# A sample's last tile routed ahead of the prompt's output products, and the prompt's choice of tokens folded into the sample's last rounds

## The reference, cut to what matters

```python
def expert_choice_ffn(x, w_router, w_gate, w_up, w_down):
    cap = EC_FACTOR * n_tok // N_EXPERTS              # 32 for the prompt, 128 for the sample
    aff = jax.nn.softmax((xf @ w_router).astype(jnp.float32), axis=-1)
    gate, idx = lax.top_k(aff.T, cap)
    xs = xf[idx]
    hdn = jax.nn.silu(jnp.einsum('ecd,edf->ecf', xs, w_gate)) * jnp.einsum('ecd,edf->ecf', xs, w_up)
    out = jnp.einsum('ecf,efd->ecd', hdn, w_down) * gate[..., None].astype(x.dtype)
    y = jnp.zeros_like(xf).at[idx.reshape(-1)].add(out.reshape(-1, D))
```

## Time and profile before

| | us |
|---|---|
| three runs | 3067.69, 3068.52, 3072.25 |
| median | 3068.52 |
| span of the profiled execution | 3067.2 |
| PE busy | 2904.8 |
| DVE busy | 2115.9 |
| ACT busy | 1578.3 |
| POOL busy | 500.5 |

### The profile page before, as it was taken

One profiled execution on the slowest core, in us unless ns is written; L12 is line 12 of the kernel. 1 busy time (PEld: TensorE's weight loads), 2 busy tenths in 40 slices (PEclk: granted clock), 3 DMA queues, 4 the chain that ended last, 5 costly groups with the idle time before them and its releaser, 6 DMA issues. The chain is left out here.

```text
span 3067.2 us, 50918 instructions
## 1 busy us (share of the span) xinstructions
PE 2904.8 (95%) x19782; PEld 2722.8 (89%) x19782; DVE 2115.9 (69%) x3420; ACT 1578.3 (51%) x2728; POOL 500.5 (16%) x477
## 2 busy tenths in 40 slices
PE   7999999989988899958999999999999999999997
PEld 5888888978877778848999999999999999999997
DVE  7212225767788566677778777877787778778887
ACT  2111214655445333316666666666676666667774
POOL 2000110013544333311000000000000000001122
PEclk9999999999999999978999999999999999999999
DMA  6478864745645544337888888888888788879894
GB/s 223 156 211 253 265 193 117 231 163 196 219 146 192 169 166 134 124 131 222 255 255 269 259 251 260 263 260 250 260 263 263 246 266 271 265 247 319 277 303 143
DMA packets 530958, 686.64 MB, mean 224 GB/s; under 512 B 18729, under 2 KB 456504, under 8 KB 525600
## 3 DMA queue, kind: packets, MB, share of 16 engines
q1 hardware_dynamic: 514816, 627.96, 63.9%
q0 software_dynamic: 15904, 55.44, 6.9%
HBM read 577.46 MB, written 105.88 MB: 223 GB/s over the span
## 5 line engine op out<-in xcount | busy, mean ns | idle before, releaser
L2515 DVE TENSOR_TENSOR moe_low<-pieces_ring,moe_high 128x1024 fp32r<-128x1024 f32 x768 | 929.8, 1222 | 156.7 <-ACT moe_high L2418 154.7
L2418 ACT ACTIVATE moe_high<-pieces_ring 128x1024 fp32r<-128x1024 f32 x768 | 796.1, 1052 | 34.8 <-PEq L103 34.8
L2365 PE MATMUL moe_down<-moe_hdn,moe_high 128*128 128x320 f32 x1920 | 510.0, 347 | 8.2 <-DVE moe_outT L2551 3.9
L2365 PE MATMUL moe_gate<-moe_xT,moe_high 128*128 128x320 f32 x1792 | 481.8, 345 | 0.9 <-DVE moe_xT L2520 0.9
L2365 PE MATMUL moe_up<-moe_xT,moe_high 128*128 128x320 f32 x1792 | 473.2, 340 | 0.0
L2366 PE MATMUL moe_down<-moe_hdn,moe_low 128*128 128x160 f32 x1920 | 453.5, 236 | 0.0
L2366 PE MATMUL moe_up<-moe_xT,moe_low 128*128 128x160 f32 x1792 | 423.3, 236 | 0.0
L2366 PE MATMUL moe_gate<-moe_xT,moe_low 128*128 128x160 f32 x1792 | 423.2, 236 | 0.0
L2365 PEld LDWEIGHTS moe_down<-moe_hdn,moe_high 128*128 128x128 f32 x1920 | 361.5, 188 | 14.8 <-DVE moe_hdn L2544 7.3
L2366 PEld LDWEIGHTS moe_down<-moe_hdn,moe_low 128*128 128x128 f32 x1920 | 367.0, 191 | 0.0
L2366 PEld LDWEIGHTS moe_gate<-moe_xT,moe_low 128*128 128x128 f32 x1792 | 342.8, 191 | 0.0
(11 more groups left out here) (335 smaller groups left out, 6156.8 us busy)
## 6 DMA issues: line engine op xcount, KB each, us to landing
pieces_ring<-in_w_gate_e SPq DMA_DIRECT2D x128, 1024.0 KB
pieces_ring<-in_w_up_e SPq DMA_DIRECT2D x128, 1024.0 KB, 5.9
pieces_ring<-in_w_down_e SPq DMA_DIRECT2D x128, 1024.0 KB, 5.5
bias_fx<-xs SPq DMA_DIRECT2D x40, 1024.0 KB, 5.4
fr_raw<-in_w_in SPq DMA_DIRECT2D x16, 1024.0 KB, 9.4
ws<-fr_late_split SPq DMA_DIRECT2D x32, 512.0 KB, 4.7
bias_fw<-ws SPq DMA_DIRECT2D x32, 512.0 KB, 8.3
mo_gates<-h SPq DMA_DIRECT2D x20, 512.0 KB, 4.5
```

The source lines that it names most:

```text
L2365: nc.tensor.matmul(ps[:, 0:2 * TOK], hi, x, start=(first and k == 0), stop=False)
L2418: nc.scalar.activation(high[:, g % HI, cols], ring[:, g % RAW, cols], ACT.Copy)\
L2515: nc.vector.tensor_tensor(low[:, g % HI, cols], ring[:, g % RAW, cols], high[:, g % HI, cols].bitcast(F32), ALU.subtract).then_inc(lo_done, 1)
```

## The change

It has three parts.

1. In round t = 8 (`SAMPLE_TILES`) the transposes of the normed rows of tile 7, its logits and its `turn_aff` are made ahead of the transposes of the mixed rows, of the second half's mixing products and of the output products of tile 8; `units` gives out the banks in that order, ACT copies x1 ahead of the mixed rows, and DVE brings `centre` and `shift` of tile 7 ahead of the weighing of tile 9. So the sample's probabilities are complete in round 8 and not in round 9.
2. DVE makes 36 of the sample's picks in the mixing stage (17 before), in groups between its other work, from round 8 on; six of them stand behind the last `keep`.
3. The prompt's probabilities go to lanes 64 to 79 of `affT`, columns 0 to 255; the other 256 columns of these lanes are set to -1 by one more memset. From pick 36 on, the picks work on lanes 0 to 79 and not 0 to 47, so the prompt's four rounds are the sample's last four. The choose stage makes only the picks 36 to 46. The prompt's list is copied to the pair backwards and goes through the same two transposes.

The diff shows, in this order: the layout and the picks, the banks, PE, ACT, POOL and DVE of the mixing stage, DVE of the choose stage.

```diff
-AFF_ROWS, AFF_COLS = 32 + NE, SEQS[0][1] + SEQS[1][1] // 2
+AFF_ROWS, AFF_COLS = 64 + NE, SEQS[1][1] // 2
+SAMPLE_ROWS, PROMPT_AT = 32 + NE, 64
 def aff_place(t):
-    second = t * P >= AFF_COLS
-    return (32, t * P - SEQS[1][1] // 2) if second else (0, t * P)
+    prompt, col = t * P < SEQS[0][1], t * P - SEQS[0][1]
+    return (PROMPT_AT, t * P) if prompt else (32 * (col // AFF_COLS), col % AFF_COLS)
-SAMPLE_TILES, EARLY_PICKS = SEQS[1][1] // P, 17
-def pick(nc, n, row, best, at, first_col):
+SAMPLE_TILES, PICKS = SEQS[1][1] // P, 3 * CAPS[1] // 8
+EARLY_PICKS = PICKS - 3 * CAPS[0] // 8
+def pick(nc, n, affT, best, at):
     r, op = divmod(n, 3)
-    lanes, cols = slice(0, row.shape[0]), slice(first_col + 8 * r, first_col + 8 * r + 8)
+    lanes, cols = slice(0, SAMPLE_ROWS if n < EARLY_PICKS else AFF_ROWS), slice(8 * r, 8 * r + 8)
+    row = affT[lanes, :]
...
-            units += [("mix", t, n) for n in range(2)] if 0 <= t < NT else []
-            units += [("x1", t - 1, n) for n in range(2)] if 0 <= t - 1 < NT else []
+            turns = [("mix", t, n) for n in range(2)] if 0 <= t < NT else []
+            sums = [("x1", t - 1, n) for n in range(2)] if 0 <= t - 1 < NT else []
+            units += sums + turns if t == SAMPLE_TILES else turns + sums
...
-                    if 0 <= t - 2 < NT:
+                    if 0 <= t - 2 < NT and t - 2 != SAMPLE_TILES - 1:
                         turn_aff(t - 2)
...
+                    if t == SAMPLE_TILES:
+                        turn_x1(t - 1)
                     if 0 <= t < NT:
                         for n in range(2):
                             pe.wait_ge(added, 2 * t + n + 1)
                             turn(("mix", t, n), mixt[:, half_of(n)], m_turned)
-                    if t + 1 < NT:
+                    if t == SAMPLE_TILES:
+                        logits(t - 1)
+                        mix(t + 1, 1, (0,))
+                        turn_aff(t - 1)
+                        mix(t + 1, 1, (1,))
+                    elif t + 1 < NT:
                         mix(t + 1, 1)
...
+                    if t == SAMPLE_TILES:
+                        copy_x1(t - 1)
+                        copy_mix(t)
+                        exp(t - 1)
+                        scale(t - 1)
+                        continue
...
+                nc.gpsimd.memset(affT[PROMPT_AT:AFF_ROWS, SEQS[0][1]:AFF_COLS], -1.0).then_inc(affT_cleared, 1)
...
-                for t in range(0, NT - 1):
+                for t in range(0, SAMPLE_TILES):
...
+                t = SAMPLE_TILES
+                add_up(t - 1, 1)
+                gather_stats(t - 1)
+                keep(t - 2)
+                o_low(t + 1)
+                centre(t - 1)
+                shift(t - 1)
+                weigh(t + 1, 0, 0)
+                weigh(t + 1, 0, 1)
+                m_low(t)
+                find_max(t - 1)
+                normalise(t - 1)
+                weigh(t + 1, 1, 0)
+                keep(t - 1)
+                pick_sample(0, 3)
+                weigh(t + 1, 1, 1)
+                pick_sample(3, 8)
+                add_up(t, 0)
+
                 t = NT - 1
+                pick_sample(8, 14)
                 add_up(t - 1, 1)
                 gather_stats(t - 1)
                 m_low(t)
                 centre(t - 1)
                 shift(t - 1)
-                keep(t - 2)
-                pick_sample(0, 4)
+                pick_sample(14, 16)
                 add_up(t, 0)
-                pick_sample(4, 9)
+                pick_sample(16, 22)
                 add_up(t, 1)
                 gather_stats(t)
                 centre(t)
                 find_max(t - 1)
                 shift(t)
                 normalise(t - 1)
+                pick_sample(22, 26)
                 keep(t - 1)
-                pick_sample(9, 15)
+                pick_sample(26, 28)
                 find_max(t)
-                pick_sample(15, 16)
+                pick_sample(28, 29)
                 normalise(t)
-                pick_sample(16, EARLY_PICKS)
+                pick_sample(29, 30)
                 keep(t)
+                pick_sample(30, EARLY_PICKS)
...
-                for row, first_col, begin, end in ((affT[0:NE, 0:n_prompt], 0, 0, 3 * CP // 8 - 1),
-                                                   (affT[:, n_prompt:AFF_COLS], CP, EARLY_PICKS, 3 * CS // 8 - 1)):
-                    for n in range(begin, end):
-                        if steps:
-                            dve.wait_ge(chain, steps)
-                        pick(nc, n, row, best, at, first_col).then_inc(chain, 1)
-                        steps += 1
-                dve.wait_ge(chain, steps)
-                nc.vector.tensor_copy(at_f[0:NE, 0:CP], at[0:NE, 0:CP]).then_inc(found, 1)
                 nc.vector.memset(pair[:], 0.0).then_inc(cleared, 1)
+                for n in range(EARLY_PICKS, PICKS - 1):
+                    if n > EARLY_PICKS:
+                        dve.wait_ge(chain, n - EARLY_PICKS)
+                    pick(nc, n, affT, best, at).then_inc(chain, 1)
...
+                prompt, last = slice(PROMPT_AT, AFF_ROWS), slice(CS - 1, CS - 1 - CP, -1)
+                nc.vector.tensor_copy(pair[prompt, 0, 0:CP], best[prompt, last]).then_inc(paired, 1)
+                nc.vector.tensor_copy(pair[prompt, 1, 0:CP], at[prompt, last]).then_inc(paired, 1)
```

More of the change, by code:

```diff
@@ L1595, in out, with turn_x1 @@
                     last.then_inc(out_done, 1)
+                def turn_x1(t):
+                    pe.wait_ge(x1_done, t + 1)
+                    for n in range(2):
+                        turn(("x1", t, n), x1_sb[:, half_of(n)], x1_turned)
                 def logits(t):
@@ L1635, in _ @@
                         out(t, 0)
[L1636 to L1639, removed]
+                    if 0 <= t - 1 < NT and t != SAMPLE_TILES:
+                        turn_x1(t - 1)
                     if 0 <= t < NT - 1:
@@ L1643, in _ @@
                         out(t, 1)
-                    if 0 <= t - 1 < NT:
+                    if 0 <= t - 1 < NT and t != SAMPLE_TILES:
                         logits(t - 1)
@@ L1739, in _ @@
                 nc.gpsimd.memset(affT[:], 0.0).then_inc(affT_cleared, 1)
+                pool.wait_ge(affT_cleared, 1)
+                nc.gpsimd.memset(affT[PROMPT_AT:AFF_ROWS, SEQS[0][1]:AFF_COLS], -1.0).then_inc(affT_cleared, 1)
+                pool.wait_ge(affT_cleared, 2)
                 pool.wait_ge(half_made, 1)
@@ L1894, in pick_sample @@
                             dve.wait_ge(picked, n)
-                        pick(nc, n, affT[:, SEQS[0][1]:AFF_COLS], best, found_at, CAPS[0]).then_inc(picked, 1)
+                        pick(nc, n, affT, best, found_at).then_inc(picked, 1)
                 def keep(t):
@@ L1900, in keep @@
                     if t == 0:
-                        dve.wait_ge(affT_cleared, 1)
+                        dve.wait_ge(affT_cleared, 2)
                     nc.vector.tensor_copy(affT[experts_of(t), col:col + P], at[experts_of(t), :]).then_inc(aff_copied, 1)
@@ L1963, in _ @@
                         normalise(t - 1)
+                t = SAMPLE_TILES
+                assert t == NT - 2
+                add_up(t - 1, 1)
[15 more added lines that the diff above has]
+                add_up(t, 0)
                 t = NT - 1
+                pick_sample(8, 14)
                 add_up(t - 1, 1)
@@ L2019, in stage_choose @@
     (_, n_prompt), (first_sample, n_sample) = SEQS
-    assert AFF_ROWS == 32 + NE and AFF_COLS == n_prompt + n_sample // 2 and first_sample == n_prompt
+    assert AFF_COLS == n_sample // 2 and first_sample == n_prompt <= AFF_COLS
     with ExitStack() as ctx:
         s = Stage(nc, ctx, "choose")
-        at_f = s.sb("at_f", [AFF_ROWS, TOK])
         pair = s.sb("pair", [AFF_ROWS, 2, CS])
         taken, first = s.sb("taken", [P, 2, NE]), s.sb("first", [P, NE], U8)
[L2026 to L2029, removed]
+        tp = s.ps("tp", [P, 2, AFF_ROWS])
+        cleared, chain, paired, turned, made = (s.sem(n) for n in ("cleared", "chain", "paired", "turned", "made"))
         with nc.Block() as block:
@@ L2055, in _ @@
+                dve.wait_ge(chain, PICKS - 1 - EARLY_PICKS)
                 dve.wait_ge(cleared, 3)
-                nc.vector.tensor_copy(pair[0:NE, 0, :], best[0:NE, CP:TOK]).then_inc(paired, 1)
-                nc.vector.tensor_scalar(pair[0:NE, 1, :], at[0:NE, CP:TOK], float(first_sample), None, ALU.add)\
+                nc.vector.tensor_copy(pair[0:NE, 0, :], best[0:NE, :]).then_inc(paired, 1)
+                nc.vector.tensor_scalar(pair[0:NE, 1, :], at[0:NE, :], float(first_sample), None, ALU.add)\
@@ L2058, in _ @@
                   .then_inc(paired, 1)
[L2059 to L2062, removed]
+                second, back = slice(32, SAMPLE_ROWS), slice(CS - 1, None, -1)
+                nc.vector.tensor_copy(pair[second, 0, :], best[second, back]).then_inc(paired, 1)
@@ L2063, in _ @@
```

(19 more changed lines are left out.)

1 line of the change is left out of this document (removed).

## The result

The changed kernel took 3058.6 us (median of 7 runs, 3057.15 to 3062.96) beside 3070.2 us of the kernel before (median of 7); the ratio is 0.9966, 95% interval 0.9957 to 0.9976, so 10.4 us less (7.4 to 13.2), and the sign is sure; the medians differ by 11.6 us. The forecast was 3057.3 us, range 3053.5 to 3062.0. In the profiled execution the span is 3059.1 us, in a run of 3062.23 us, one of the two longest. Two executions of one kernel differ by some us before they reach the edited place: PE's transposes of the heads of tile 9, the last ones ahead of the first reordered instruction, start at 1297.05 us in the profile before and at 1297.72 in this one.

A forecast was written before the change was run, and what follows sets the result against it. DVE's serial pick chain between two barriers bounds the choose stage, while PE bounds nearly everything else. Terms -5.40 - 14.53 + 0.3 + 7.4 + 1.0 = -11.2 us take 3068.5 to 3057.3 us, range 3053.5 to 3062.

The forecast's parts named there:

- The choose stage loses 19.6 us: Choice of tokens between two barriers: 5.40 us of prompt rounds and 14.53 of sample picks go, small pieces add 0.3.
- lanes are free: Choose stage: picks on 80 lanes cost nothing extra; the rival that lanes cost 3.0 us more had chance 0.03.
- The mixing stage gains 7.4 us: Mixing stage with 19 more picks: last keep 2.8 us later plus six uncovered picks of 4.6; bounds 6.2 to 9.0.
- The stall for the shared bank: Mixing round 8: PE's transposes wait for ACT's x1 copies to free the tp banks, losing 0.65 us.
- the sum 0.4 us late: Mixing round 8: six picks end at 1324.3, after the next sum's product at 1323.9, delaying that sum 0.4 us.
- the last keep behind four picks: Mixing round 9: four picks (3.1 us) precede keep of tile 8, so the last logits start at 1347.65, not 1345.18.
- The rival in which the picks hide nowhere: Each of the 19 moved picks lengthens the mixing stage, 14.5 us not 7.4: about -4.1, 3064.4 us; chance 0.05.
- The clock stays: Before the last output product PE waits some 1.9 us, for 1.41 before, without its clock falling.
- The clock rival: PE's clock falls before the last output product, costing 2.3 us: -8.9, 3059.6 us; chance 0.06.
- The gather costs 1.0 us more: Expert stage's start: the first gather flies beside the preload's rest, +1.0 us on 5.0, bounds -0.8 and +2.5.
- The rival "stands behind the preload": Expert stage's start: the gather moves only after the preload ends, +2.5 us: -9.7, 3058.8 us; chance 0.05.
- The slower rival: Expert stage is paced by its stream of pieces, which starts 7.4 us later: 3075.9 us; chance 0.03.

The follow-up runs named there:

- fold_only: Kernel before with the prompt's lanes joined to the sample's last four rounds, mixing stage order and 17 early picks unchanged: 3064.5 us, ratio 0.9985.
- late_picks: Changed kernel with all 36 early picks moved behind the last keep: 3081.4 us, ratio 1.0037 to the kernel before.
- keep_first: Changed kernel with keep of tile 8 placed ahead of picks 22 to 25, not behind them: 3058.7 us in a single run.
- hold6: Changed kernel with all six pieces preloaded, but pieces 6 and 7 held until the gather has landed: 3060.1 us in a single run.
- late_stream: Changed kernel with no preload in the choose stage, all six pieces issued at the expert stage's start: 3063.5 us, ratio 0.9978 to the kernel before.
- the two timings: Changed kernel against the kernel before, timed twice without further edit: 3058.6 us, ratio 0.9966, and 3059.2 us, ratio 0.9971.
- the two parts: Kernel before with only the prompt's lanes joined (3064.5 us), and with only the new mixing order and 36 early picks (3062.5 us).
- hold3: Changed kernel with three of six pieces preloaded in the choose stage, the other three issued after the first gather landed: 3057.2 us, ratio 0.9965.

## Why the prediction held, and which term was off

- *The choose stage loses 19.6 us.* It went from 32.16 to 12.47 us, 19.7 less. The rates of a pick by kind were right, lanes are free (fold_only), and the copies and transposes at its end were sized rightly.
- *The mixing stage gains 7.4 us.* It gained 62.15 - 54.90 = 7.25. The stall for the shared bank (0.65 taken; in late_picks, where no pick delays it, the sum stands 0.69 us later from the mark than before), the sum 0.4 us late (0.39 against late_picks), the last keep behind four picks and six uncovered picks are all there. Late_picks shows that 21 us of picking are hidden, keep_first that 1.2 of the delay came from one order of two calls. The rival in which the picks hide nowhere falls.
- *The clock stays.* PE waited 1.91 us ahead of the last output product and the window over it shows a granted clock of 1.00 (2.4 GHz). The clock rival falls.
- *The gather costs 1.0 us more.* This term was mis-sized: 3.15 us, and above the bound of 2.5. I had taken the bounds from later gathers, beside which SP issues single pieces, for one that meets a full queue. That the preload causes it is shown: 4.35 us as soon as half of it is held back, and no other part of the path to the first product moved by more than 0.1 us. The rival "stands behind the preload", with 2.5, came nearest in size, but its mechanism holds only in part: the gather did wait behind packets issued before it, 1.58 MB of them in hold6, but not behind the whole preload, and in late_stream it landed ahead of a piece issued before it. Nor did it share from its issue on, as the forecast had it. The Trainium skill (DMA: Bandwidth & Descriptors, Queues, rings and completion order) says that a DMA engine takes turns between queue rows, packet by packet. The trace agrees for the time in which both queues move, 116 packets to 131, and doesn't show it in the 4.6 us ahead of the gather's first packet. Why the first packet comes so late stays open.
- *The stream is not the bound.* The preload started 7.25 us later and the stage behind it was as long; in late_stream another 12.4 us later, the same. The slower rival falls.

With the gather at its measured size the sum is -19.7 + 7.25 + 3.15 = -9.3 us, which is what the trace shows up to the first product and agrees with 10.4 and 8.9 us of the two timings. The forecast of 11.2 was 1.9 us too large: 2.15 for the gather, and 0.2 the other way for the rest. That the measured median lies 1.3 us from the forecast one is in part luck: the interval of the timing holds both 11.2 and 9.3, and only the traces tell them apart.

## What to carry to other kernels

A serial chain on one engine between two barriers is worth its full length, and it can be taken apart into the gaps of the stage before if each group is no longer than the wait that covers it; write down for each wait what the engine does behind it, and let what another engine waits for go first. When a stage is shortened, look at what ran beside it: here the preload no longer fitted under the choice, and of the two parts' 13.2 us 3.55 were lost to a small gather that then met it. Preload only as much as lands before the next urgent transfer.

## What the runs showed of the hardware that was not expected

A gather of 160 rows of 4 KB (two indirect DMAs, counted from the second's issue) needs 4.3 to 5.0 us from issue to use on idle or nearly idle DMA engines, and 8.1 to 8.5 us beside a queue of 1 MB loads at 346 GB/s, although its own 0.66 MB are only 1.9 us of that rate. Nearly all of the difference is a wait ahead of its first packet (5.0 us from issue in hold6, 1.7 in hold3). Once it moves, it is hardly slowed: it takes about every second packet, and its packets are four times as large. Loads issued behind it added nothing measurable (8.10 us in one run without them, 8.15 to 8.23 with them).
